# A mixer's first product, for ten of its twelve column groups, with the weights standing and the activations streaming

## The reference

```
h = rmsnorm(x, g[0])                       # x * r * g, r per token
z = h @ w_in                               # 2048 -> 6144 columns
x0, x1, v = split(dwconv3(z[:, :3072], hy_short_w, hy_short_b))
y_a = x0 * two_sided_fftconv(v * x1, h_fwd, h_bwd, hy_bias)
gb, gc, xv = split(z[:, 3072:])
y_b = gb * dwconv3(gc * xv, sc_conv_w)
m = concat([y_a, y_b]) @ w_out
```

## Time and profile before

| | |
|---|---|
| median of 3 runs | 2268.82 us (2268.69 to 2268.94) |
| span of the profiled execution | 2266.9 us, so 1.9 us less than the runs' median, which also holds what lies around it |
| PE busy | 2255.3 us, 99% of the span |
| DVE busy | 1675.5 us, 74% |
| ACT busy | 1332.9 us, 59% |
| w_z's first product to w_mo's first | 7.21 to 305.70 us |

### The profile page before, as it was taken

How to read it: one execution, slowest core, us unless ns; L and a number is a source line. 1 busy time by engine, 2 the same in 40 slices (tenths; PEclk the granted TensorE clock), 3 DMA queues, 4 the chain that set the end, 5 groups by cost and what they waited for, 6 DMA issues and landing times.

```text
span 2266.9 us, 26633 instructions
## 1 busy us (share of the span) xinstructions
PE 2255.3 (99%) x10625; PEld 1873.7 (83%) x10625; DVE 1675.5 (74%) x2025; ACT 1332.9 (59%) x1775; POOL 104.5 (5%) x138
## 2 busy tenths in 40 slices
PE   9999999999999999999999999999999999999998
PEld 7778888888888888888888888888888888888887
DVE  6676864887788788787878788778788685456664
ACT  6455444766666666666666666666666564444443
POOL 0000000000000000000000000000000010000000
PEclk9999999999999999999999999999999999999999
DMA  9454455899998999886578999989888645643343
GB/s 358 167 174 162 164 186 186 289 291 272 287 303 265 277 292 267 283 282 236 219 281 240 287 289 261 285 281 277 270 281 258 240 152 223 244 172 149 148 163 116
DMA packets 77132, 542.63 MB, mean 239 GB/s; under 512 B 8682, under 2 KB 9013, under 8 KB 13968
## 3 DMA queue, kind: packets, MB, share of 16 engines
q1 hardware_dynamic: 61568, 429.58, 50.2%
q0 software_dynamic: 15296, 111.23, 22.7%
q10 hardware_dynamic: 144, 0.12, 0.0%
HBM read 534.60 MB, written 6.29 MB: 239 GB/s over the span
## 4 chain that ended last, share of the span: by engine, by line
PE 98%; DVE 2%; issue 0%; ACT 0%; ACTq 0%; POOLq 0%; POOL 0%
PE P L359 95%; PE P L362 3%; DVE low L626 0%; DVE R_h L614 0%; DVE R_f L611 0%; DVE R_f_r L611 0%; DVE R_g L614 0%; DVE X L614 0%; ACT R_h L502 0%; ACT EV L533 0%; DVE st L614 0%; DVE R_f L708 0%; ACT X L502 0%; DVE X L611 0%; ACTq L2710 0%
## 5 line engine op out<-in xcount | busy, mean ns | idle before, releaser
L626 DVE TENSOR_TENSOR low<-raw,hi 128x1024 fp32r<-128x1024 f32 (+3 forms) x694 | 813.4, 1200 | 290.7 <-ACT hi L507 286.4
L507 ACT ACTIVATE hi<-raw 128x1024 fp32r<-128x1024 f32 (+3 forms) x694 | 704.5, 1040 | 463.5 <-PE P L359 309.5
L359 PE MATMUL P<-hi,R_h 128*128 128x512 f32 (+2 forms) x2944 | 944.2, 392 | 0.6 <-DVE R_h L614 0.6
L359 PE MATMUL P<-hi,R_f_r 128*128 128x512 f32 x2480 | 791.4, 391 | 0.1
L359 PEld LDWEIGHTS P<-hi,R_h 128*128 128x128 f32 x2944 | 552.3, 188 | 116.4 <-issue 5.8
L359 PE MATMUL P<-low,R_h 128*128 128x512 f32 (+2 forms) x1472 | 570.2, 387 | 0.0
L359 PEld LDWEIGHTS P<-hi,R_f_r 128*128 128x128 f32 x2480 | 465.6, 188 | 96.3 <-DVE R_f_r L611 0.3
L359 PE MATMUL P<-low,R_f_r 128*128 128x512 f32 x1240 | 482.5, 389 | 0.0
L626 DVE TENSOR_TENSOR low<-R_f,hi 128x1024 fp32r<-128x1024 f32 x226 | 267.7, 1221 | 82.9 <-ACT hi L507 82.2
L359 PEld LDWEIGHTS P<-low,R_h 128*128 128x128 f32 x1472 | 276.7, 188 | 54.7 <-issue 2.6
L359 PEld LDWEIGHTS P<-low,R_f_r 128*128 128x128 f32 x1240 | 233.0, 188 | 47.1
(11 more groups left out here) (229 smaller groups left out, 1406.2 us busy)
## 6 DMA issues: line engine op xcount, KB each, us to landing
raw<-in_w_d SPq DMA_DIRECT2D x128, 1024.0 KB, 7.2
R_f<-in_w_u POOLq DMA_DIRECT2D x84, 1024.0 KB, 10.5
raw<-in_w_u SPq DMA_DIRECT2D x72, 1024.0 KB, 5.6
raw<-in_w_z SPq DMA_DIRECT2D x45, 1024.0 KB, 4.9
raw<-in_w_i SPq DMA_DIRECT2D x36, 1024.0 KB, 4.9
R_f<-in_w_u SPq DMA_DIRECT2D x28, 1024.0 KB, 6.9
X<-in_w_u SPq DMA_DIRECT2D x28, 1024.0 KB, 8.7
raw<-in_w_mo SPq DMA_DIRECT2D x16, 1024.0 KB, 4.9
```

The costliest lines, as they stand in the source:

```text
L359: return self.e.matmul(o, l, r, start=start, stop=stop, skip_group_check=True)
L507: self.e.activation(hi, raw, ACT.Copy).then_inc(*self.inc("high_made", ("high", k, d)))
L626: self.e.tensor_tensor(low, raw, hi.bitcast(f32), ALU.subtract).then_inc(*self.inc("low_made", *lows))
```

## The change

The first two groups (gc) stay as they are. In the other ten, a weight tile holds all 2048 input channels of 128 columns. Now a block of weights stands in PE and h streams: for each of 16 blocks one matmul of the high weights with HH and HL side by side (2 x 256 columns, one instruction) and one of the low weights with HH (256 columns). The result already has channels on partitions, so there are no evacuation with r and no turns. It lies in two parts in one bank (columns 0 to 255 and 256 to 511). gathered copies the second part (ACT), adds the first (DVE) and multiplies by r along the tokens (DVE), except for xv. For that, r is made into a row on all partitions once: norm_diagonal writes diag(r) and ones (DVE), norm_spread multiplies them on PE, a copy lands the row in STAT. The groups gc get r squared instead of r, for gc and xv together. column_pair takes two tiles and calls step three times a tile: after blocks 0 to 3, after 8 to 11 and at its end. The work behind a pair goes to later as two pieces: gathering with the middle tap (or the gate), then the side taps (rest).

```
-    o["w_z"] = tile_w(np.concatenate([w[:, 512 * g:512 * g + 512] for g in Z_ORDER], 1), 512)
+    rows = tile_w(np.concatenate([w[:, 512 * g:512 * g + 512] for g in Z_ORDER[:Z_ROWS]], 1), 512)
+    cols = np.concatenate([w[:, 512 * g:512 * g + 512] for g in Z_ORDER[Z_ROWS:]], 1)
+    o["w_z"] = np.concatenate([rows, tile_w(cols, 128, 16)], 0)
...
+PAUSES = 0, 2
...
+        self.H_both = v3(R_h[:, :], 2)
+        self.r_row, self.r_square = self.STAT[:, 0:256], st[:, 40:42]
...
+    def column_product(self, b, wh, wl, j, ks, x_ready, free, *done):
+        m = self.m
+        o = m.P[b]
+        for k in ks:
+            self.wait_ge(x_ready)
+            self.wait_ge(("low", j, k // 4))
+            both, high = m.H_both[:, :, 256 * k:256 * k + 256], m.HH[:, k, :]
+            if k == 0:
+                self.wait_ge(free)
+            if k < 15:
+                self.mm(o[:, :], wh[:, k, :], both, k == 0, False)
+                last = self.mm(o[:, 0:256], wl[:, k, :], high, False, False)
+            else:
+                self.mm(o[:, 0:256], wl[:, k, :], high, False, False)
+                last = self.mm(o[:, :], wh[:, k, :], both, False, True)
+        if done:
+            last.then_inc(*self.inc("product_done", *done))
+
+    def norm_spread(self, b, k, ready, free, done):
+        m = self.m
+        self.wait_ge(free)
+        self.wait_ge(ready)
+        for t in range(2):
+            last = self.mm(m.P[b][:, 128 * t:128 * t + 128], m.EV[k][:, 256:384], m.EV[k][:, 128 * t:128 * t + 128], True, True)
...
+    def gathered(self, k, banks, row, ready, row_ready, free, done):
+        self.wait_ge(free)
+        for d, b in enumerate(banks):
+            self.wait_ge(ready[d])
+            self.copy(self.m.EV[k][:, 256 * d:256 * d + 256], self.m.P[b][:, 256:512], (done, "copied", d))
...
+    def gathered(self, k, banks, row, ready, row_ready, free, done):
+        m = self.m
+        o = m.EV[k]
+        for d, b in enumerate(banks):
+            part = o[:, 256 * d:256 * d + 256]
+            self.wait_ge((done, "copied", d))
+            self.tt(part, m.P[b][:, 0:256], part, ALU.add, (done, "half", d))
+        if row is not None:
+            self.wait_ge(row_ready)
+            self.wait_ge((done, "half", 1))
+            z = v3(o[:, :], 2)
+            self.tt(z, z, row.unsqueeze(1).to_broadcast([128, 2, 256]), ALU.mult, done)
+
+    def norm_diagonal(self, k, ready, free, done):
+        m = self.m
+        self.wait_ge(free)
+        self.e.memset(m.EV[k][:, 256:384], 1.0).then_inc(*self.inc("dve_done"))
+        self.wait_ge(ready)
+        self.tt(m.r_square, m.R1, m.R1, ALU.mult, (done, "square"))
+        for t in range(2):
+            self.ts(m.EV[k][:, 128 * t:128 * t + 128], m.ident[:, :], m.R1[:, t:t + 1], None, ALU.mult, done)
...
+    def mixer_columns(kind, c, banks, products):
+        k, done = ev(hold=True), mark("gathered")
+        by_row = kind != "xv"
+        E.gathered(k, banks, m.r_row if by_row else None, products, norm_m["row"], ev_free[k], done)
+        for d in range(2):
+            bank_free[banks[d]] = [(done, "half", d)]
...
             if kind == "v":
+                kv, vx = ev(hold=True), mark("vx")
+                ds = [EV[kv][:, 256 * d:256 * d + 256] for d in range(2)]
+                ends, taps = conv(zs, ds, ws, bs, whole, [ev_free[kv]] * 2, True)
+
+                def rest():
+                    taps()
+                    E.gated_v(c, ds, ends, [g0_m[c], g0_m[c + 1]], vx)
...
         else:
+            done = gate(z, z, G1[:, c:c + 2, :], [whole, g1_m[c], g1_m[c + 1]])
             g1_m[c] = g1_m[c + 1] = done
+            mix_m[c] = mix_m[c + 1] = plain_parts(MH[:, c:c + 2, :], ML[:, c:c + 2, :], z, [done, list(k_names)])
+            let_go(k, mix_m[c])
+            rest = nop
+        return rest
...
+    def column_pair(kind, c):
+        banks, products = pair(), []
+        for d in range(2):
+            j, wh, wl = take("w_z")
+            wh, wl = v3(wh, 16), v3(wl, 16)
+            done = ("product", j, 1)
+            for part, ks in enumerate((range(0, 4), range(4, 8), range(8, 12), range(12, 16))):
+                whose = {1: [("used", j, 0)], 3: [done, ("used", j, 1)]}.get(part, [])
+                E.column_product(banks[d], wh, wl, j, ks, list(h_m), bank_free[banks[d]], *whose)
+                if part in PAUSES:
+                    step()
+            products.append(done)
+            release(j, done)
+            step()
+        rest = []
+        later.extend([lambda: rest.append(mixer_columns(kind, c, banks, products)), lambda: rest[0]()])
 
     for n, kind in enumerate(kinds):
-        banks, done = gemm("w_z", HH, HL, h_m, 16, 512, steps=2)
-        flush()
+        if n < Z_ROWS:
+            banks, done = gemm("w_z", HH, HL, h_m, 16, 512, steps=2)
+            flush()
+            if n == 0:
+                norm_diagonal()
+            ks, ms = evac(banks, done, scale=m.r_square, scale_m=norm_m["square"])
+            later += [nop] * 4 if n == 0 else [nop]
+            for c in (0, 2):
+                later.append(lambda c=c + 4 * n, ks=ks, ms=ms: row_turn(c, ks, ms))
+            if n == 1:
+                later.append(norm_spread)
+            continue
+        for c in (0, 2):
+            column_pair(kind, c + 4 * (n % 2))
         if n == 7:
             flush_all()
-        ks, ms = evac(banks, done, scale_m=list(r1_m))
-        later += [nop] * {0: 4, 1: 1, 8: 1, 9: 1, 10: 1}.get(n, 0)
-        for c in (0, 2):
-            later.append(lambda kind=kind, c=c + 4 * (n % 2), ks=ks, ms=ms: mixer_turn(kind, c, ks, ms))
-        if n == 7:
             later += [nop] + [lambda t=t, g=g: vx_turn(t, g) for t in range(2) for g in range(2)]
```

More of the change, by code:

```diff
@@ L90 @@
 Z_ORDER = [8, 9, 10, 11, 2, 3, 4, 5, 6, 7, 0, 1]
+Z_ROWS = 2
 def laid_out(i):
@@ L347 @@
         cmp_values_out = cols_ready = compress = copy_out = copy_turned = double = filter_hidden = filter_out = \
-        filter_sums = final_row = final_scale = finish = first_load = first_table = gate = \
+        filter_sums = column_product = gathered = final_row = final_scale = finish = first_load = first_table = gate = \
         gated_silu = gated_v = gates = half_dft = half_silu = halved_rstd = halves = head_columns = inverse = load_piece = load_tile = \
         masked_exp = memory_out = mla_out = nsa_out = ones_row = plain_exp = plain_parts = padded_keys = pool_scale = pool_windows = \
-        product = norm_mean = norm_part = norm_whole = norm_root = relu_square = residual = rope = rope_keys = scale = scaled_parts = scores = side_load = side_taps = sine = sine_of = \
+        product = norm_mean = norm_part = norm_diagonal = norm_spread = norm_whole = norm_root = relu_square = residual = rope = rope_keys = scale = scaled_parts = scores = side_load = side_taps = sine = sine_of = \
         split_high = split_low = square_sum = store = tile_sum = chain_load = chain_add = combine = operand_sum = times_row = times_row_apart = pads = group_sums = tail_keys = tail_rows = turn = v_times_k = values = warm = y_back = idle
@@ L373, in product @@
             last.then_inc(*self.inc("product_done", *done))
+    def column_product(self, b, wh, wl, j, ks, x_ready, free, *done):
[21 more added lines that the diff above has]
+            last = self.mm(m.P[b][:, 128 * t:128 * t + 128], m.EV[k][:, 256:384], m.EV[k][:, 128 * t:128 * t + 128], True, True)
+        last.then_inc(*self.inc("turn_done", done))
     def warm(self, b, k, n, zero, done):
@@ L1686, in conduct, with conv @@
     g0_m, g1_m = [None] * 8, [None] * 8
-    def conv(zs, dsts, ws, biases, ready, frees):
+    def conv(zs, dsts, ws, biases, ready, frees, apart=False):
         done = mark("conv")
         E.centre(zs, dsts, ws, biases, ready, frees, done)
+        ends = [(done, d) for d in range(len(zs))]
+        if apart:
+            return ends, lambda: E.side_taps(zs, dsts, ws, done)
         E.side_taps(zs, dsts, ws, done)
-        return [(done, d) for d in range(len(zs))]
+        return ends
     def gate(o, z, g, ready, free=None):
@@ L1697, in gate, with row_columns, norm_diagonal, norm_spread @@
         return done
-    def mixer_columns(kind, c, b, turned):
-        z = v3(P[b][:, :], 2)
+    def row_columns(c, b, turned):
+        done = mark("gc")
+        E.copy_out(G0[:, c:c + 2, :], v3(P[b][:, :], 2), turned, list(h_m), done)
+        g0_m[c] = g0_m[c + 1] = done
+        bank_free[b] = [done]
+    norm_m = {}
+    def norm_diagonal():
+        norm_m["k"] = k = ev(hold=True)
+        norm_m["diagonal"] = done = mark("diagonal")
+        norm_m["square"] = (done, "square")
+        E.norm_diagonal(k, [list(r1_m), id_m[1]], ev_free[k], done)
+    def norm_spread():
+        b, k, done = bank(), norm_m["k"], mark("spread")
+        norm_m["row"] = mark("row")
+        E.norm_spread(b, k, norm_m["diagonal"], bank_free[b], done)
+        let_go(k, done)
```

(44 more changed lines are left out.)

## The result

The changed kernel takes 2279.94 us (median of 5 runs, 2279.33 to 2280.34) against 2268.82 (5 runs). The ratio is 1.0049, 95% interval 1.0038 to 1.0059: 11.1 us slower, 7.3 us above the forecast and 0.9 us above the range. The profiled span is 2278.2 us, 11.3 longer.

The account below looks back on a forecast made before the run. The prediction took PE to bound the kernel, with 98% of the chain of waits. Its terms -5.1 + 3.1 + 0.2 + 5.6 gave +3.8 us, so 2268.8 became 2272.6 us, range 2264 to 2279.

Parts of the forecast that it names:

- PE alone, -5.1: PE's own work in the changed stage: turns removed -9.7, new products +4.2, norm_spread +0.4, together -5.1 us.
- +4.2: PE's new weight tiles: 16 steps of 0.2267 + 0.120 us make 5.55 instead of 5.44; 40 tiles cost +4.2 us.
- Rival E: In the new tiles' steps, alternating widths or the two-piece operand cost 10 ns a step, 6.4 us more; 2278 us, chance 0.13.
- First place: At the turn of v in tile 32, PE waits 3.1 us for the gated v; bounds 2 to 5 us.
- Second place: At tile 40, PE waits 5.6 us because DVE's queue, with v times the filter, takes 44.3 against 38.7 us.
- Third place: At the filter's kernels, filter_4 on DVE near tile 22's bank: cost 0, up to 2 us if misjudged.
- The 0.2 for v_dft: At v_dft, PE waits another 0.2 us for the last of four turned copies.
- C: DVE keeps up, so the wait at tile 40 vanishes: 2267.0 us, chance 0.18.
- D: The gated v is ready too at its turn, so no wait is left: 2263.7 us, chance 0.10.
- forecast A: Main case for the changed stage: PE's own work plus the waits, +3.8 us, giving 2272.6 us; chance 0.33.
- rival B: PE's clock falls in the wait at tile 40, costing 2.6 us more: 2275.2 us, chance 0.26.
- w_mo's first product after 314: Sign that the prediction is wrong: w_mo's first product starting before 307 us or after 314 us.

Follow-up runs that it names:

- experiment 6: Changed kernel with HH and HL interleaved by blocks, so the wide product streams 512 neighbouring columns: 2279.55 us, ratio 1.0048.
- experiment 8: Experiment 7 with two wide then two narrow products: 2266.50 us; with four and four: 2267.37 us.
- Experiment 7: Changed kernel with three more empty steps before v's turn, empty steps around each v_times_k and four ahead of y_back: 2267.51 us, ratio 0.9995.
- experiment 2: Changed kernel with an empty step ahead of each v_times_k and one behind it: 2272.19 us, ratio 1.0015.
- experiment 4: Changed kernel with unread products keeping PE busy, 12 ahead of v's first turn and 20 ahead of tile 40: 2276.83 us, ratio 1.0035.
- experiment 3: Changed kernel with three more empty steps before v's turn and empty steps around each v_times_k: 2271.77 us, ratio 1.0012.
- experiment 9: Changed kernel with two side steps per weight tile instead of three: 2291.21 us, ratio 1.0100.
- experiment 5: Changed kernel with the wide product first in all 16 steps of a tile, the last included: 2280.22 us, ratio 1.0049.

## Why the prediction was right and wrong

**PE alone, -5.1.** The turns went as counted; the step did not. 0.2267 + 0.120 = 0.347 comes from stretches of one width each; the mixed steps take a mean of 0.3514. The term "+4.2" is 3.0 us too small (640 x 0.0047). Rival E had the place and twice the size, 6.4, but its causes are not borne out: the two-piece operand costs nothing (experiment 6), and the number of changes of width does not order the steps (experiment 8). The cause of the 3.0 us stays open. Experiment 7 checks the corrected sum without long waits: its list of waits is 0.7 us longer than that of the kernel before, so -5.1 + 3.0 + 0.7 is -1.4; its span is 1.3 below that of before.

**First place, 3.1.** Measured 3.2, with the chain as written. PE got there at 207.45, not near 204; the forecast counted both sides from tile 31's last product, so the later hour moved both. **Second place, 5.6.** Measured 5.2, at tile 40, on the add that frees its bank; the denser issue as the cause is shown by experiment 2. Both sides of the sum were right: from v_dft's first product at 221.29, PE wanted tile 40 after 39.6 us (forecast 38.7) and got it after 44.8 (44.3). **Third place, 0.** No wait there. The 0.2 for v_dft does not stand in the list either. Rivals C and D fall.

**Failed: the lower clock at nothing.** The step that failed is the sum of forecast A, which priced two waits and put what follows them at nothing; rival B, the clock in the second wait, had less chance and 2.6 us. The clock fell behind both waits. Behind the first it cost 1.5 us (the change against experiment 6), behind the second 3.0 by the windows; experiment 4 measured 4.3 for both by the start of w_mo. B's price was right for its place; that it would also fall behind the 3.2 us wait, no rival had. Nor had any rival the clock and the slower steps together. The forecast's own sign, w_mo's first product after 314, came true at 317.48.

The Trainium skill (TensorE: Matmul & The Clock Gate, Part 1) says that PE, idle for long enough, runs at half speed until it has been busy again. The windows agree for the second wait: 0.50 from 266 to 270, behind 5.18 us of idling, and 1.00 from 274 on.

**The account**: -5.1 + 3.0 (steps) + 3.2 + 5.2 (waits) + 1.5 + 3.0 (lower clock) = +10.8; the span grew by 11.3. The remaining 0.5 is not assigned. The forecast's +3.8 lacked 3.0 for the steps and 4.5 for the clock; either alone would have left the time within the range. It ranked the cases as if a wait and its after-effect were alternatives, when one can follow from the other.

**Not foreseen**: y_back as the third place. It shows only when the first two are mended (experiment 3), or the steps are fewer (experiment 9).

## What to carry to other kernels

When side work is issued by steps, moving the steps moves every reader's deadline: list each reader on PE with what it waits for, and after mending one look for the next (here the turn of v, tile 40, y_back, in this order). Price a wait of PE with what comes after it: here 3.2 us cost up to 4.7, and 5.2 cost some 8. And take a product's cost from rows with the same sequence of widths; where there are none, 5 ns a step times 640 steps is 3 us.

## What the hardware showed that was not expected

Behind a wait of 3.2 us the granted clock fell to 1.2 GHz in the change and in experiment 3 (0.58 from 288 to 292), but not in experiment 6, where it was as long (1.00 from 212 to 216). Nor is the fall the same each time. In the change the window from 208 to 212 has 0.82. In experiment 2, whose instructions are the same up to there, it still has 1.00, though PE was back at work at 210.81; the next one has
```profile
212.00:216.00 4.00, 4.00 (x17) 3.50 (x16) 3.35 (x4) 2.66 (x4) 0.00 (x0) 0.57 0.01 4
```
In experiment 5 the lower level lasted longer behind the same wait (0.79, 0.50 and 0.85 in the windows from 208 to 220). And the four runs of experiment 6 make two pairs: 2278.56 and 2278.81 with a mean clock of 0.998, 2280.28 and 2280.45 with 0.997. They lie 1.6 us apart, about the price of one fall behind this wait. So it seems that one and the same kernel has the fall in one execution and not in another; what decides no run here shows.

Alternating products of 512 and 256 columns start in two patterns within one kernel. PE's timeline of the changed kernel:
```profile
166.01 0.39 PE L365 MATMUL P<-R_h,hi 128*128 128x512 f32 x1
...
168.44 0.39 PE L365 MATMUL P<-R_h,hi 128*128 128x512 f32 x1
...
169.83 0.40 PE L365 MATMUL P<-R_h,hi 128*128 128x512 f32 x1
...
171.95 0.40 PE L365 MATMUL P<-R_h,hi 128*128 128x512 f32 x1
```
Seven steps of 0.347 lie in the first two lines, six of 0.353 in the last two, with nothing but the end of a tile between them. The slower pattern is the commoner one; its cause is open.
